# Halving two layer norms by token kind, with latent projection pieces ahead, in a one-core two-layer diffusion backbone

## What is computed

```
x = x + g2 * _rms_norm(ffn(h2), norm_g[3])              # end of layer 0; the same for ctx
h = _modulate(_rms_norm(x, norm_g[0]), sh1, sc1)        # start of layer 1
hc = _modulate(_rms_norm(ctx, norm_g[0]), csh1, csc1)
q_lat = _diff_q(z[..., :DIFF_WIDTH], rope)              # z = h @ w_in, latent rows
k_ctx, v_ctx = _diff_kv(hc @ w_in[:, DIFF_WIDTH:3 * DIFF_WIDTH], None)
d_lat = _fourier(z[..., 3 * DIFF_WIDTH:])               # latent rows
```

## Time and profile before

| | |
|---|---|
| median of 3 runs | 1743.98 us (1741.13 to 1744.02) |
| the profiled execution | 1743.9 us |
| its span in the trace | 1742.3 us |
| mean granted TensorE clock | 0.976 |
| TensorE matmul busy | 1667.6 us (96%) |
| VectorE busy | 1056.1 us (61%) |
| ScalarE busy | 939.1 us (54%) |
| instructions | 22952 |

### The profile page before, as it was taken

How to read it: one execution, slowest core, us unless ns; L and a number is a source line. 1 busy time by engine, 2 the same in 40 slices (tenths; PEclk the granted TensorE clock), 3 DMA queues, 4 the chain that set the end, 5 groups by cost and what they waited for, 6 DMA issues and landing times.

```text
span 1742.3 us, 22952 instructions
## 1 busy us (share of the span) xinstructions
PE 1667.6 (96%) x8514; PEld 1324.1 (76%) x8514; DVE 1056.1 (61%) x1354; ACT 939.1 (54%) x1341; POOL 37.8 (2%) x60
## 2 busy tenths in 40 slices
PE   6998999899999999989979899999999999999997
PEld 3785458888888888668847788888888888888885
DVE  2441232353222333354284799999998989999997
ACT  3512333362222222362265577777787777777775
POOL 0000000030000000000000100000000000000000
PEclk8898899999999999989999999999999999999999
DMA  7523375169222232353204799999999999999982
GB/s 304 200 97 140 132 283 194 65 249 403 98 99 97 84 110 99 117 196 112 79 1 194 290 420 364 389 369 398 353 414 361 397 369 383 386 374 374 375 345 71
DMA packets 67706, 426.25 MB, mean 245 GB/s; under 512 B 8624, under 2 KB 12464, under 8 KB 19760
## 3 DMA queue, kind: packets, MB, share of 16 engines
q1 hardware_dynamic: 59856, 396.93, 59.5%
q0 software_dynamic: 7776, 28.32, 4.2%
HBM read 401.62 MB, written 23.59 MB: 244 GB/s over the span
## 4 chain that ended last, share of the span: by engine, by line
PE 90%; DVE 3%; ACT 3%; DMA 2%; issue 1%; SPq 0%; DVEq 0%; ACTq 0%
PE ps L1553 25%; PE ps L1555 25%; PE ps L1554 25%; PE ps L1571 3%; PE ps L1595 2%; PE ps L1710 2%; DMA raw<-in_w 1%; PE ps L1604 1%; PE ps L1974 1%; PE ps L1759 1%; DVE small L1141 1%; PE ps L1741 1%; ACT raw L515 1%; DMA cst<-in_cst 1%; ACT ah L518 1%
## 5 line engine op out<-in xcount | busy, mean ns | idle before, releaser
L1407 DVE TENSOR_TENSOR wl<-raw,wh 128x1024 fp32r<-128x1024 f32 x522 | 615.3, 1221 | 62.9 <-ACT wh L860 56.1
L860 ACT ACTIVATE wh<-raw 128x1024 fp32r<-128x1024 f32 x522 | 523.0, 1053 | 97.3 <-PE ps L1555 97.3
L1553 PE MATMUL ps<-ah,wh 128*128 128x512 f32 (+1 forms) x848 | 303.1, 357 | 10.0 <-DVE al L969 5.4
L1553 PE MATMUL ps<-wh,ah 128*128 128x512 f32 (+1 forms) x800 | 309.5, 387 | 1.0 <-issue 0.4
L1555 PE MATMUL ps<-wh,al 128*128 128x512 f32 (+1 forms) x800 | 302.3, 378 | 0.0
L1554 PE MATMUL ps<-wl,ah 128*128 128x512 f32 (+1 forms) x800 | 302.0, 377 | 0.0
L1554 PE MATMUL ps<-al,wh 128*128 128x512 f32 (+1 forms) x848 | 295.0, 348 | 0.0
L1555 PE MATMUL ps<-ah,wl 128*128 128x512 f32 (+1 forms) x848 | 295.0, 348 | 0.0
L939 DVE TENSOR_TENSOR wl<-raw,wh 128x1024 fp32r<-128x1024 f32 x120 | 141.4, 1221 | 93.0 <-ACT wh L472 93.0
L1553 PEld LDWEIGHTS ps<-ah,wh 128*128 128x128 f32 x848 | 162.7, 192 | 34.9 <-issue 7.3
L1554 PEld LDWEIGHTS ps<-al,wh 128*128 128x128 f32 x848 | 162.8, 192 | 21.2 <-issue 1.5
(11 more groups left out here) (252 smaller groups left out, 1578.1 us busy)
## 6 DMA issues: line engine op xcount, KB each, us to landing
raw<-in_w SPq DMA_DIRECT2D x372, 1024.0 KB, 6.9
sent<-raw POOLq DMA_DIRECT2D x16, 512.0 KB, 24.0
back<-raw POOLq DMA_DIRECT2D x16, 512.0 KB, 25.0
x<-sent POOLq DMA_DIRECT2D x7, 512.0 KB, 12.3
back<-x POOLq DMA_DIRECT2D x7, 512.0 KB, 9.3
x<-in_x SPq DMA_DIRECT2D x1, 2048.0 KB, 11.5
raw<-in_ukv SPq DMA_DIRECT2D x1, 1024.0 KB, 7.3
out<-x SPq DMA_DIRECT2D x4, 256.0 KB, 2.5
```

What stands on the lines that cost most here:

```text
L860: act.activation(wh[:, J % SPLITS, piece_half(h)], slot(J % SLOTS)[:, piece_half(h)], ACT.Copy).then_inc(w_hi, 1)
L1407: ins = dve.tensor_tensor(wl[:, J % SPLITS, piece_half(h)], slot(J % SLOTS)[:, piece_half(h)], wh[:, J % SPLITS, piece_half(h)].bitcast(F3 ...
L1553: pe.matmul(out, lh, rh, start=start, stop=False)
```

## The change

Both norms between the layers are done in two halves: `N_EFL` and `N_O1L` for the 256 latent columns, `N_EFC` and `N_O1C` for the context columns, the latter with their sums in bank 5. VectorE now evicts all eight banks (4 to 7 first, then 0 to 3, these after ScalarE's fourth latent square). TensorE's queue becomes: 8 sums of `N_EFL`, 2 of `N_EFC`, modulation 40, 6 of `N_EFC`, 8 of `N_O1L`, modulation 41 and 42, then the projection. The Fourier piece moves from place 9 to place 3, so that pieces 0 to 3 need latent columns only; keys are 4 to 6, values 7 to 9. Modulation 43 and 44 stand inside piece 0, 45, 46 and 47 behind pieces 0, 1 and 2, and the ring is ordered to fit. The sums of `N_O1C` stand behind piece 1 and inside piece 2, and its modulated chunks are first read by piece 4. In ScalarE's program the copies of pieces 1 and 2 out of PSUM (`project`) stand among the squares and the chunks of `N_O1C`. The router shift moves behind piece 4. The first Fourier matmuls move behind piece 7, with banks 6 and 7, and ScalarE copies them before it copies piece 9; the second Fourier matmuls stay behind piece 9. The scores no longer wait for the Fourier remainder; the attention waits for it at its third step.

```diff
+OIN_COLUMNS = (0, 1, 2, 9, 3, 4, 5, 6, 7, 8)
...
+    if M_OIN <= i < M_OOUT:
+        i = M_OIN + OIN_COLUMNS[i - M_OIN]
...
-            + mods(GAP_MODS, N_MOD) + main(M_OIN + 2, MAIN))
-
-
-ROWS_AT = {0: GAP_MODS + 2, 1: GAP_MODS + 3, 3: GAP_MODS + 4, 5: GAP_MODS + 5, 7: GAP_MODS + 6}
+            + mods(GAP_MODS, GAP_MODS + 5) + main(M_OIN + 2, M_OIN + 3) + mods(GAP_MODS + 5, GAP_MODS + 6) + main(M_OIN + 3, M_OIN + 4)
+            + mods(GAP_MODS + 6, N_MOD) + main(M_OIN + 4, MAIN))
...
+OIN_F, OIN_K, OIN_V, OIN = 3, 4, 7, 10
...
+NORM_COLS = {N_EYL: LATENT, N_E2L: LATENT, N_EYC: CONTEXT, N_E2C: CONTEXT, N_EFL: LATENT, N_EFC: CONTEXT, N_O1L: LATENT,
+             N_O1C: CONTEXT, N_OY: LATENT, N_O2: LATENT}
+NORM_BANK = {N_EYC: 5, N_E2C: 5, N_EFC: 5, N_O1C: 5}
...
+           + [e for k in range(KD) for e in ((N_E2L, k), (N_EYC, k))] + each(N_E2C)
+           + each(N_EFL) + each(N_EFC)[:2] + each(N_O1L) + each(N_EFC)[2:] + each(N_O1C) + each(N_OY))
+ROOTS = [N_E1, N_Q, N_KV, N_EYL, N_E2L, N_EYC, N_E2C, N_EFL, N_EFC, N_O1L, N_O1C, N_OY, N_O2]
...
-            root(N_O1)
-            rows(N_MOD - 1)
-            for k in range(KD):
-                modulate(N_O1, 1, 0, 0, k, tmp[k % 2])
-
-
-            for p in range(10):
-                s = M_OIN + p
-                split(s + 2)
-                act.wait_ge(w_used, s + 1)
+            def sub_square(k, half):
+                n = N_EFC if half else N_EFL
+                if half or k >= 4:
+                    act.wait_ge(sem("y2_dve"), (3, 3, 4, 4, 1, 1, 2, 2)[k])
+                    square(n, k, y2_e[:, k, cols_of(n)])
+                else:
+                    square(n, k, ps[:, k, cols_of(n)])
+
+            def next_square(n, k):
...
+            for k in range(KD):
+                sub_square(k, 0)
+            sub_square(0, 1)
+            sub_square(1, 1)
+            root(N_EFL)
+            rows(GAP_MODS)
+            for k in range(2, KD):
+                sub_square(k, 1)
+            for k in range(KD):
+                next_square(N_O1L, k)
+                if k == 5:
+                    root(N_EFC)
+            root(N_O1L)
+            rows(GAP_MODS + 1)
+            for k in range(KD):
+                modulate(N_O1L, 1, 0, 0, k, tmp[k % 2])
+                if k in (0, 4, 7):
+                    rows(GAP_MODS + 2 + (k + 1) // 4)
+            split(M_OIN + 2)
+            project(0)
+            rows(GAP_MODS + 5)
+            for k in range(4):
+                next_square(N_O1C, k)
+            split(M_OIN + 3)
+            for k in range(4, KD):
+                next_square(N_O1C, k)
+                if k == 5:
+                    project(1)
+                    rows(GAP_MODS + 6)
+            root(N_O1C)
+            for k in range(KD):
+                modulate(N_O1C, 1, 0, 0, k, tmp[k % 2])
+                if k == 3:
+                    project(2)
+                    rows(N_MOD - 1)
+                    split(M_OIN + 4)
+            project(OIN_F)
...
+            for p in range(OIN_K, OIN):
+                split(M_OIN + p + 1)
+                if p == 9:
+                    act.wait_ge(sem("four_ps"), 1)
+                project(p)
+            split(M_OIN + OIN + 1)
             act.wait_ge(sem("four_ps"), 2)
...
-            for q in range(2, 4):
+            for q in (2, 3, 0, 1):
+                if q < 2:
+                    dve.wait_ge(sq_ready, SQ_AT[N_EFL, 3] + 1)
                 dve.tensor_copy(y2_e[:, 2 * q:2 * q + 2, :], ps[:, 2 * q:2 * q + 2, :]).then_inc(sem("y2_dve"), 1)
...
+            inverse(N_EFL)
+            sub_residual(N_EFL, range(KD))
+            inverse(N_EFC)
+            sub_residual(N_EFC, range(2))
+            modulate(N_O1L)
+            sub_residual(N_EFC, range(2, 4))
+            split(M_OIN + 2)
+            sub_residual(N_EFC, range(4, KD))
             dve.wait_ge(res_done, 4 * KD)
             dve.memset(small[:, 9:10], 0.0).then_inc(sem("y2_used"), 1)
-            modulate(N_O1)
+            split(M_OIN + 3)
+
+            def beside(k):
+                if k == 4:
+                    split(M_OIN + 4)
+
+            modulate(N_O1C, beside)
             dve.wait_ge(sem("mod_cols"), N_MOD)
             take_modulation(1, GAP_MODS - MOD_LAYER0, N_MOD - MOD_LAYER0)
...
-            for p in range(10):
+            for p in range(OIN_F, OIN):
                 split(M_OIN + p + 2)
-                if p == 7:
+                if p == 5:
                     dve.wait_ge(sem("shift_logits"), 1)
                     dve.tensor_copy(shift_logits, ps[:, 6, 0:NE]).then_inc(sem("shift_taken"), 1)
+                if p == 7:
...
+                t = p - OIN_F
+                if t < 6:
+                    dve.wait_ge(sem("orope_ps"), t + 1)
...
             pe.wait_ge(sem("y2_dve"), 1)
-            sum_squares(N_EF)
+            sum_squares(N_EFL)
+            sum_squares(N_EFC, range(2))
             pe.wait_ge(sem("y2_dve"), 2)
             mod_piece(GAP_MODS)
-            for n in range(GAP_MODS + 1, GAP_MODS + 4):
-                filler(n)
-            for k in range(KD):
-                sum_square(N_O1, k)
-                if k % 2:
-                    filler(GAP_MODS + 4 + k // 2)
-            mod_cols(N_MOD - 1)
-
-
...
+            sum_squares(N_EFC, range(2, KD))
+            sum_squares(N_O1L)
+            filler(GAP_MODS + 1)
+            filler(GAP_MODS + 2)
+            pe.wait_ge(sem("y2_dve"), 4)
...
+                pe.wait_ge(evac_act, evacs(("i", t if t < 3 else t - 3 + OIN_K), "act"))
-            for p in range(10):
-                W = T if 3 <= p < 6 else TL
-                piece(M_OIN + p, W, (lambda k: pe.wait_ge(mod_lo, MOD_BEFORE[N_O1] + k + 1)) if p == 0 else None, tokens=(6 <= p < 9))
...
+            def latent_chunk(k):
+                pe.wait_ge(mod_lo, MOD_BEFORE[N_O1L] + k + 1)
+                if k in (2, 5):
+                    filler(GAP_MODS + 2 + (k + 1) // 3)
+
+            def context_sum(k):
+                if 2 <= k < 6:
+                    sum_square(N_O1C, k + 2)
+
+            def context_chunk(k):
+                pe.wait_ge(mod_lo, MOD_BEFORE[N_O1C] + k + 1)
+
+            for p in range(OIN):
+                piece(M_OIN + p, T if OIN_K <= p < OIN_V else TL, {0: latent_chunk, 2: context_sum, OIN_K: context_chunk}.get(p), tokens=p >= OIN_V)
+                if p == 1:
+                    sum_squares(N_O1C, range(4))
+                if p < 3:
+                    filler(GAP_MODS + 5 + p)
+                if p == 3:
+                    mod_cols(N_MOD - 1)
+                if OIN_F <= p < OIN_F + 6:
+                    turn(p - OIN_F)
+                if p == 4:
                     pe.wait_ge(sem("router_shift"), 1)
                     pe.wait_ge(sem("last_scales"), 1)
                     pe.matmul(ps[:, 6, 0:NE], ones, router_shift, start=True, stop=True).then_inc(sem("shift_logits"), 1)
-
-            pe.wait_ge(sem("dftc_loaded"), 16)
...
-            mm.then_inc(sem("four_ps"), 1)
+                if p == 7:
+                    pe.wait_ge(sem("dftc_loaded"), 16)
+                    pe.wait_ge(sem("dftt_loaded"), 16)
+                    pe.wait_ge(evac_act, evacs(("i", OIN_F), "act"))
+                    pe.wait_ge(sem("shift_taken"), 1)
+                    for t in range(2):
+                        for c in range(2):
+                            mm = pe.matmul(ps[:, 6 + t, c * 256:(c + 1) * 256], f_o[:, c, t * P:(t + 1) * P], dftc, start=True, stop=True)
+                    mm.then_inc(sem("four_ps"), 1)
+
...
-            pe.wait_ge(sem("four_lo"), 1)
+            pe.wait_ge(evac_act, evacs(("i", OIN - 1), "act"))
             pe.wait_ge(sem("orope_done"), 6)
-            pe.wait_ge(sem("shift_taken"), 1)
...
             def early_norms(i):
+                if i == 2:
+                    pe.wait_ge(sem("four_lo"), 1)
```

More of the change, by code:

```diff
@@ L1238, in _, with sub_residual @@
             dve.wait_ge(sem("rows_cleared"), 16 * 4 * NE)
-            for q in range(2, 4):
+            for q in (2, 3, 0, 1):
+                if q < 2:
+                    dve.wait_ge(sq_ready, SQ_AT[N_EFL, 3] + 1)
                 dve.tensor_copy(y2_e[:, 2 * q:2 * q + 2, :], ps[:, 2 * q:2 * q + 2, :]).then_inc(sem("y2_dve"), 1)
-            dve.wait_ge(sem("y2_act"), 2)
-            dve.wait_ge(sem("y2_dve"), 2)
-            residual(N_EF, lambda k: y2_e[:, k, :], 0, 3)
+            dve.wait_ge(sem("y2_dve"), 4)
+            def sub_residual(n, chunks):
+                cols = cols_of(n)
+                for k in list(chunks) + [None]:
+                    if k is not None:
+                        if k >= 2:
+                            dve.wait_ge(res_done, RES_BEFORE[n] + k - 1)
+                        normed(n, y2_e[:, k, cols], tmp[k % 2][:, cols], k)
+                    before = (k if k is not None else chunks[-1] + 1) - 1
+                    if before in chunks:
+                        residual_add(n, 0, 3, before, tmp[before % 2][:, cols])
+            inverse(N_EFL)
```

(15 more changed lines are left out.)

75 lines of the change are left out of this document (29 added, 46 removed).

## The result

| | before | after |
|---|---|---|
| median | 1742.59 us (1741.13 to 1744.02, 6 runs) | 1732.44 us (1730.68 to 1736.41, 6 runs) |
| ratio | | 0.994, 95% interval 0.993 to 0.9951 |
| profiled execution, span | 1742.3 us | 1730.9 us |
| last down matmul ends | 722.0 | 720.9 |
| first score reduction starts | 871.0 | 858.1 |

What follows compares the result with a forecast made beforehand. TensorE was taken as the bound (99.91 of 100 us in the experts' loop). The stretch from last down matmul to first score reduction falls from 149.0 to 137.2; 11.8 off 1743.9 gives 1732.1 us, range 1727.0 to 1738.5.

Steps and rivals of the forecast that it cites:

- Rival D: Experts' loop: the 11.8 us won before the attention are lost at expert loads, 1744; chance 0.07 including gain-eaten low clock.
- The half norms: Norms between the layers: first 24 half-width sums take 15.4 us, pairs about 1.17 apart; the last eight 4.0.
- Latent piece first: Input piece 0 starts at 742 behind the latent sums, with about 0.9 us of waits replacing 6.6 + 2.45.
- Context modulation: Beside pieces 1 to 3: costs nothing, ready for piece 4 at 779 with 1 us to spare.
- Rival A: Piece 45's load or piece 4's split is late by 2.2, low clock 3.0 follows: 1737.3 us; chance 0.17.
- Spread: Modulation pieces spread: piece 43's 2.2 us load wait goes; piece 45's load lands at 751, needed at 752.
- Clock: Behind the wait for modulation piece 43: the lower granted clock's cost, 3.0 us, goes with the wait.
- rivals B and C: Low clock in the sums: B eats the gain, 1744 (0.07 including Rival D); C persists through piece 0, about 1755 (0.03).
- Fourier: Tail behind piece 9: moving the first half earlier removes 3.2 us of copy waits; 0.2 of VectorE subtraction stays.
- The sum: Last down matmul to first score reduction: all terms add to 137.2 us against 149.0, 11.8 less.
- the 0.7 that I couldn't place: Same stretch before the change: 0.7 of its 19.7 us beyond TensorE's own work was unexplained and left in.
- The rule against: VectorE tiles should have at least 512 elements: two halves cost 0.84 us against 0.69, a loss by that rule alone.

Runs made afterwards that it cites:

- run 5: Changed kernel with four half-wide square buffers in place of two for the half norms: stretch 132.7 us against 137.2, median 1728.30 us.
- Run 3: Changed kernel with the context residuals, sums and root ahead of the first latent chunk again, halves and spread kept: stretch 140.3 us, median 1737.49 us.
- run 4: Changed kernel with four unused 512-column copies on ScalarE ahead of the split of input piece 4: stretch 138.3 us, median 1733.71 us.
- Run 2: Changed kernel with all eight modulation pieces ahead of input piece 0 again: stretch 147.25 us, median 1741.69 us.
- run 9: Unread small matmuls added in TensorE's standstills: kernel before, stretch 146.4 us, median 1742.51; kernel before with the spread alone, 145.3 us, 1740.67.
- run 1: Changed kernel with the Fourier part alone put back behind input piece 9: stretch 139.7 us, median 1733.54 us.
- runs 2 and 8: Run 2, and the kernel before with the spread of the modulation pieces alone: the latter's stretch 146.2 us, median 1741.07 us.
- run 7: Kernel with four square buffers and early split of piece 57, plus modulation pieces moved among the sums: stretch 132.3 us, median 1728.67 us.

## Why the prediction was right, point by point

- **Where.** All of the gain is in the stretch that was named, and it keeps its size to the end of the experts' loop. Rival D is out.
- **The half norms.** 24 sums took 15.9 for a predicted 15.4: a pair comes at 1.26 us (eight sums in 5.06, from 722.17 to 727.23), not 1.17, and 0.42 and 0.81 of waiting show at the roots. The mechanism was right and the term 0.5 short; run 5 shows it (take the hand-off away and 0.46 a sum is left). No run undoes the halves themselves, so what halving alone brings is not measured.
- **Latent piece first.** Piece 0 started 21.4 us behind the last down matmul for a predicted 20.2: 0.5 from the sums, 0.7 from fillers 41 and 42 with their turns (3.2, not 2.5; two pieces at 1.0 and two turns at 0.5 are 3.0 by the prediction's own figures, a slip in the start but not in the sum). Piece 0 with its two modulation pieces took 9.9 (742.31 to 752.17) for 9.6 (5.7 + 3.0 + 0.9): only one wait of 0.4 is marked, but the 0.9 was needed in full, as the first product behind each change of work holds TensorE longer (0.20 for 0.12). Run 3 gives the order 3.1 us.
- **Context modulation.** Piece 4 at 779.0 as predicted (the base lies 1.1 lower, so 1.1 later by length). Its split had 1.0 us to spare, measured by run 4. Rival A's condition was as close as stated and wasn't met.
- **Spread.** No wait for a load, piece 45's included (at 752.17, predicted 752), so the 2.2 are gone. Run 2 shows that the others rest on it: with all eight pieces in front 10 of the 11.8 us are gone.
- **Clock.** 3.0 predicted for the low clock, 2.6 shown by run 9, since 0.4 turns into a wait for the next load. In the sums, with marked waits of 0.2 to 0.8 us, it stayed at 1.00: rivals B and C are out. The Trainium skill, TensorE: Matmul & The Clock Gate, describes in its second failure mode a clock that oscillates through micro-idles; no window of the sums shows that.
- **Fourier.** 3.2 predicted with 0.2 back; run 1 gives 2.5. The step that was missed is what is late next: the split of piece 57 and the Fourier remainder on VectorE, which end the stretch.
- **The sum.** Piece 4 started 58.1 us behind the last down matmul for a predicted 57, 1.1 late, all of it there before piece 0 begins. From there to the first reduction it took 79.1 for 80.2, 1.1 early: the 0.7 that I couldn't place didn't return, the two Fourier halves hold TensorE for 1.54 and 3.55 us (827.34 to 828.88, 852.94 to 856.49) in place of 1.98 and 3.73, and the scores with what is behind them took 1.57 for 1.35. So 137.2 twice is partly luck; the terms are good to half a microsecond or so.
- **The end.** The span is 11.4 shorter, not 11.8: 1.1 more was gained ahead of the stretch, where the last down matmul ends anywhere from 719.2 to 723.2 in the profiled executions of kernels that differ only behind it, 0.3 between the stretch and the end of the loop, and 1.8 lost at the end, 1.6 of it where the matmuls ran at the lower clock.
- **The time.** 1732.1 against a median of 1732.44 is luck in part too. The base, 1743.9, was one execution and 1.3 above the median of six; from 1742.6 the same 11.8 us would have given 1730.8, and the medians show 10.2. The upper bound of the range, 1738.5, also lies below the 1739.1 that the prediction worked out itself.
- **The rule against.** Two products of 256 did cost VectorE 0.42 each where one of 512 took 0.69. The Trainium skill, VectorE: DVE Perf Modes, on the fixed extra latency of SBUF sources, speaks of such a cost per instruction, and the trace agrees. The stretch became shorter all the same, because TensorE was the one that waited.

The undone parts sum to 2.5 + 3.1 + 10.05, more than 11.8: they don't add, as the parts cover each other. That halves and spread need each other is shown from both sides (runs 2 and 8); how the 11.8 would be divided between them has no single answer.

## What to carry to other kernels

Where one engine is full nearly everywhere, list its standstills and what its own work is in each; what a reorder can win is the standstills, and what it must not do is move work to where the engine is full (run 7). When a chain is split into halves, double the buffers between the engines with it: two more were worth 4.5 us here, for one changed wait and the buffers' unused halves. In a ring of n slots, work that uses a slot each must stand far enough apart for a load to land between a use and the use n later, and a transfer that is late can cost twice, by its wait and by the clock behind it (2.2 and 2.6 us in the kernel before).

## What the runs showed that I had not expected

- Small matmuls that nobody reads, put into standstills of 2.2 to 4.8 us, went with a granted clock of 1.00 in the wait and in the work right behind it in all four kernels. In the stretch, where the clock had fallen in both kernels without them, that was worth 2.6 and 0.9 us. At the end the eight matmuls were 2.6 us shorter with four buffers, but there some kernels run them fast without help.
- The same standstill at the end of the kernel (3.1 to 3.7 us) left the eight matmuls behind it at 3.7 us in five kernels and at 5.3 to 6.4 us in seven others. Differences of 2 us between kernels are to be read from a stretch, not from the total.
- The time of a group as the timeline gives it can hold a wait: the first product of piece 4 shows 0.80 us where it was free to start and 0.50 where it followed a wait.
